# Order and placement of the three partial products of each weight tile in a float32 decoder layer

## The reference

```python
def decoder_layer(x, pos, ret_S0, rwkv_S0, shift0, p):
    x = x + 0.5 * swiglu(rms_norm(x, p['norm_ffn1']), p['ffn1_w_gu'], p['ffn1_w_down'])
    h = rms_norm(x, p['norm_mix'])
    z = h @ p['w_in']
    ...
    ret_S, o_ret = retention_branch(zq, zk, zv, zg, pos, ret_S0)
    rwkv_S, o_rwkv, shift = rwkv7_branch(zs, shift0, rwkv_S0, p)
    merged = (jax.nn.sigmoid(zgr) * (o_ret @ p['w_ret_o'])
              + jax.nn.sigmoid(zgw) * (o_rwkv @ p['w_rwkv_o']))
    x = x + merged @ p['w_out']
    x = x + 0.5 * swiglu(rms_norm(x, p['norm_ffn2']), p['ffn2_w_gu'], p['ffn2_w_down'])
    return x, ret_S, rwkv_S, shift
```

## Time and profile before

| | us |
|---|---|
| Median of 3 runs | 2866.72 |
| Lowest, highest | 2866.03, 2868.74 |
| The profiled execution | 2868.76 |
| Its span, first to last instruction | 2867.0 |

### The profile page before, as it was taken

How to read it: one execution, slowest core, us unless ns; L and a number is a source line. 1 busy time by engine, 2 the same in 40 slices (tenths; PEclk the granted TensorE clock), 3 DMA queues, 4 the chain that set the end, 5 groups by cost and what they waited for, 6 DMA issues and landing times.

```text
span 2867.0 us, 57289 instructions
## 1 busy us (share of the span) xinstructions
PE 2841.1 (99%) x24662; PEld 2768.5 (97%) x24662; DVE 1564.2 (55%) x1679; ACT 1117.0 (39%) x1121; POOL 107.2 (4%) x144
## 2 busy tenths in 40 slices
PE   9999999999999999999999999999999999999998
PEld 8999999999999999898998999999999999999998
DVE  6444444444567576775865555466544444454454
ACT  5333333333344453544534644233433333333333
POOL 0000000000000002011020010000000000000000
PEclk9999999999999999999999999999999999999999
DMA  5444454444456553635436444555444445444454
GB/s 205 167 163 164 162 171 176 161 171 155 164 186 228 190 186 111 249 131 200 162 139 240 176 154 165 187 203 184 164 172 161 166 161 171 175 162 167 155 169 144
DMA packets 85460, 495.80 MB, mean 173 GB/s; under 512 B 10320, under 2 KB 10496, under 8 KB 44096
## 3 DMA queue, kind: packets, MB, share of 16 engines
q1 hardware_dynamic: 71424, 444.14, 44.0%
q0 software_dynamic: 9280, 32.72, 3.1%
q10 hardware_dynamic: 4608, 16.78, 1.5%
HBM read 462.80 MB, written 30.80 MB: 172 GB/s over the span
## 4 chain that ended last, share of the span: by engine, by line
PE 93%; DVE 3%; ACT 2%; DMA 1%; issue 0%; SPq 0%; ACTq 0%; DVEq 0%; POOLq 0%
PE psum L545 29%; PE psum L546 29%; PE psum L547 29%; PE psum L893 1%; PE psum L709 1%; DVE sb_w_lo L1506 1%; DMA sb_raw<-in_w_wo 0%; DMA sb_raw<-in_gu 0%; PE psum L666 0%; ACT sb_w_hi L1094 0%; DVE sb_w_lo L1512 0%; ACT sb_w_hi L1085 0%; PE psum L906 0%; PE psum L903 0%; PE psum L745 0%
## 5 line engine op out<-in xcount | busy, mean ns | idle before, releaser
L547 PE MATMUL psum<-sb_h,sb_w_lo 128*128 128x288 f32 x4384 | 1297.7, 296 | 0.0
L546 PE MATMUL psum<-sb_h,sb_w_hi 128*128 128x288 f32 x4384 | 1293.9, 295 | 0.0
L545 PE MATMUL psum<-sb_h,sb_w_hi 128*128 128x288 f32 x4384 | 1288.5, 294 | 4.2 <-DVE sb_w_lo L1506 1.7
L1512 DVE TENSOR_TENSOR sb_w_lo<-sb_raw,sb_w_hi 128x2048 fp32r<-128x2048 f32 (+1 forms) x348 | 712.4, 2047 | 713.8 <-ACT sb_w_hi L1085 713.2
L1085 ACT ACTIVATE sb_w_hi<-sb_raw 128x2048 fp32r<-128x2048 f32 (+1 forms) x349 | 600.2, 1720 | 1207.6 <-PE psum L547 1177.5
L545 PEld LDWEIGHTS psum<-sb_h,sb_w_hi 128*128 128x128 f32 x4384 | 828.4, 189 | 28.5 <-issue 19.9
L547 PEld LDWEIGHTS psum<-sb_h,sb_w_lo 128*128 128x128 f32 x4384 | 823.9, 188 | 0.0
L546 PEld LDWEIGHTS psum<-sb_h,sb_w_hi 128*128 128x128 f32 x4384 | 821.5, 187 | 1.3 <-issue 1.0
L547 PE MATMUL psum<-sb_g,sb_w_lo 128*128 128x288 f32 x1408 | 416.8, 296 | 0.0
L546 PE MATMUL psum<-sb_g,sb_w_hi 128*128 128x288 f32 x1408 | 415.4, 295 | 0.0
L545 PE MATMUL psum<-sb_g,sb_w_hi 128*128 128x288 f32 x1408 | 407.0, 289 | 0.0
(11 more groups left out here) (380 smaller groups left out, 2389.0 us busy)
## 6 DMA issues: line engine op xcount, KB each, us to landing
sb_raw<-in_gu SPq DMA_DIRECT2D x175, 1024.0 KB, 4.8
sb_raw<-in_down SPq DMA_DIRECT2D x128, 704.0 KB, 4.1
sb_raw<-in_w_mix SPq DMA_DIRECT2D x72, 1024.0 KB, 4.9
sb_raw<-in_w_gates SPq DMA_DIRECT2D x32, 1024.0 KB, 5.4
sb_s_ret<-in_s_ret POOLq DMA_DIRECT2D x32, 512.0 KB, 8.4
out_ret_s<-sb_s_ret ACTq DMA_DIRECT2D x32, 512.0 KB, 5.4
sb_raw<-in_w_ro SPq DMA_DIRECT2D x16, 1024.0 KB, 4.8
sb_raw<-in_w_out SPq DMA_DIRECT2D x16, 1024.0 KB, 4.8
```

Source lines behind the costliest of these rows:

```text
L545: pe.matmul(out, wh, xh, start=start, stop=False)
L546: pe.matmul(out, wh, xl, start=False, stop=False)
L547: return pe.matmul(out, wl, xh, start=False, stop=stop)
L1512: dve.tensor_tensor(w_lo[:, slot, 0:cols], raw[:, slot, 0:cols], w_hi[:, slot, 0:cols].bitcast(F32), ALU.subtract).then_inc(lo_made, 2)
```

## The change

Two things are changed. In `products` the last two matmuls change places: line 546 is now low weights by high inputs, line 547 high weights by low inputs. And the tensors are placed anew: low weights 192 bytes from the high ones modulo 256 instead of 128, high inputs 80 bytes instead of 144, and with them low inputs 208 instead of 16. To use the gaps, `h` now stands before `w_lo`, and `dend` and `gains` have moved. The tensors from `x` and `o_ret` on shift by 32 bytes up, those behind an `align` by 64 bytes down; `or_hi` stands at 160 or 32, `or_lo` at 192 or 64.

```diff
-LINES, APART = 256, 144
+LINES, APART, LOW_APART = 256, 80, 192
...
         w_hi = sb("w_hi", [P, 2, BLK], F32R)
-        eps_c = sb("eps_c", [P, 3])
-        first_root = eps_c[:, 2:3]
-        own = sb("own", [P, SB])
...
-        align(4 * T % LINES)
+        eps_c = sb("eps_c", [P, 3])
+        first_root = eps_c[:, 2:3]
+        own = sb("own", [P, SB])
+        h_hi, h_lo = halves_of("h", KT)
+        dend = sb("dend", [P, 2, 4 + SB])
+        align(LOW_APART)
         w_lo = sb("w_lo", [P, 2, BLK], F32R)
-        h_hi, h_lo = halves_of("h", KT)
+        gains = sb("gains", [P, 4, KT])
         mean_w = sb("mean_w", [P, P])
         head_w = sb("head_w", [P, P], F32R)
         ident = sb("ident", [P, P])
-        gains = sb("gains", [P, 4, KT])
         arena = place[0]
...
-        dend = sb("dend", [P, 2, 4 + SB])
...
                 pe.matmul(out, wh, xh, start=start, stop=False)
-                pe.matmul(out, wh, xl, start=False, stop=False)
-                return pe.matmul(out, wl, xh, start=False, stop=stop)
+                pe.matmul(out, wl, xh, start=False, stop=False)
+                return pe.matmul(out, wh, xl, start=False, stop=stop)
```

## The result

| | before | after |
|---|---|---|
| median, us | 2866.38 (2866.03 to 2868.74, 4 runs) | 2901.43 (2887.57 to 2913.79, 4 runs) |
| profiled execution, us | 2868.76, span 2867.0 | 2887.57, span 2885.8 |
| ratio | | 1.0119, 95% interval 1.009 to 1.0148 |

What follows compares the result with a forecast made beforehand. TensorE was taken to bound the kernel: 6560 tiles by their step, plus some 290 us. One 6.667 ns step less over 5730 tiles, 38 us, from 2866.7 gave 2828 us; whole range 2790 to 2906.

Steps and rivals of the forecast that it cites:

- The bound: Whole kernel: TensorE sets the time, 6560 weight tiles of three products times their step, plus some 290 us untouched.
- the small ones: Matmuls touched by moved small buffers and shifted mixing buffers: left at their cost, some 3 us either way.
- the first rival: Products: inputs' high, high, low cycle and places modulo 64 are kept, so 393.3 ns and 2867 us stay; chance 0.22.
- The reload: Rival, products: losing the repeated load of high weights leaves none short, 400 ns a tile, 2905 us; chance 0.15.
- the looser lost lock: Rival, products: tiles fall to the other layout's 398.4 ns, 29 us slower, 2896 us; chance 0.13.
- The forecast: Products: three different distances make a tile one step shorter, 387 ns, saving 38 us to 2828 us; chance 0.42.
- no longer meet alike: Products: input streams and loads, all 144 bytes apart before, meet at 144, 80 and 208, giving 127 + 127 + 133 ns.
- The argument from distances alone: Products: the step follows from distances modulo 256 between input stream and load; addresses matter by about 5 ns a tile.
- The grid: Products: a pattern repeating every tile moves in steps of 6.667 ns, so only 386.7, 393.3 or 400.0 ns can occur.
- The tiles between small matmuls: Mixing steps: half of 1152 tiles counted as following the pattern, making 5730 tiles in all.
- The loads: Weight loads of 187, 188, 189 ns should change with the product beside them if the streams' meeting is the cause.
- wrong in kind: Test of the whole forecast: it fails if the step varies within the stretch or the difference lies outside the three lines.

Runs made afterwards that it cites:

- the bare streams: Kernels without the layer: TensorE alone runs bursts of three-product tiles at listed addresses; before's placement took 393.3 ns a tile, the changed kernel's 395.5 or 395.6 in the first sweep.
- old/192/80: Changed kernel with the old order of products, keeping low weights at 192 and high inputs at 80; 2890.71 us, ratio 1.0081.
- new/32/16: Changed kernel in its new order, with low weights at 32 and high inputs at 16; 2849.98 us, ratio 0.9934.
- 2 of 20 bursts: Products alone without the layer, changed kernel's order and placement, 20 bursts after varying pauses: 395.5 or 395.6 ns in 15, 406.7 in 3, 386.7 in 2.
- the shift of 16 bytes: Products alone without the layer, before's placement with all four operands moved together by 16 bytes: 396.7 ns a tile in 19 bursts, 396.6 in 1.
- the second trace of the changed kernel: Changed kernel run again unchanged, also called the repeat; 2921.16 us, ratio 1.0151, profiled span 2935.2 us.
- old/48/144: Kernel before, old order and high inputs at 144, with low weights at 48 instead of 128 and small buffers moved; 2860.44 us, ratio 0.9975.
- 448 single bursts: Products alone without the layer, one burst for each of 448 placements in both orders, low inputs 128 bytes on: 148 at 400.0 ns, 106 at 393.3, 88 at 396.7.

## Why the prediction was wrong, step by step

- **The bound held.** The time is 6560 tiles by their step; nothing else moved. 18.5 of the 18.8 us lie in the three lines, and all other matmuls together moved by 0.3 us, within the 3 that I gave the small ones (line 964 gained 0.9 us, line 590 lost 0.7). VectorE and ScalarE did not change.
- **That addresses modulo 256 bytes matter held, and the first rival fell.** Its condition (places modulo 64 and the inputs' cycle are kept, so nothing changes) was met to the letter, and the step moved by 2.3 to 13.4 ns. The sentence of the Trainium skill that I had set beside it (SBUF — State Buffer, section Who interferes with whom: "PE and ACT never wait on anyone") is about one engine holding up another, and the bare streams neither confirm nor refute it, since no other engine works in them. What they refute is what I drew from it, that no placement would change a step: with every other engine idle, TensorE's step for the same three products goes from 386.7 to 406.7 ns by where its operands lie.
- **The reload fell, though the sign and size of its rival came near.** It gave 2905 us, and the looser lost lock 2896; measured was 2901. But its reason (a product is short because of the reload) is refuted from both sides: old/192/80 has the reload and no product at 289, new/32/16 lacks it and is faster than before. A time that fits is no evidence for the reason.
- **The forecast failed at the step that it called its weakest**: that three different distances would put the tile at 386.7. No row stood behind "no longer meet alike". The pattern exists at this placement (127 to 131 ns gaps, 2 of 20 bursts), but two others exist as well, and the kernel's long stretches fell into those every time in two traces: 395.6 ns in one, 406.7 in the other, where the sum had 386.7. The argument from distances alone fails too, by the shift of 16 bytes.
- **The grid was right in its unit and wrong in its period.** I took the pattern to repeat every tile, so that only 386.7, 393.3 and 400.0 could occur. It may repeat over three tiles (178 x 6.667 / 3 = 395.6) or two (390.0), so steps a third or a half of 6.667 ns apart are open, and small losses with them. What I read as "equal durations, hence one stable lock" was a property of before's placement, not of TensorE: before is one of those with a single pattern.
- **The tiles between small matmuls were mis-sized.** I counted half of 1152 as in the pattern. The 1568 tiles of the lora columns, the mixing steps and the gates paid 5.4 ns each, more than twice the 2.3 of the long stretches, and 8.5 of the 18.8 us are theirs. Short stretches at 386.7, 395.6 and 406.7 ns all occur there, so I take it that every interruption starts the choice anew, but no run separates that from what a tile loses while it settles.
- **The loads move, but not with the product beside them.** In the second trace of the changed kernel the loads of lines 545 and 546 take 193 ns, where the first trace has 188. The load of line 545 runs beside the 305 ns of line 547, that of line 546 beside the 295 ns of line 545, that of line 547 beside the 296 ns of line 546. So loads and products change together with the pattern, which fits the meeting of the two streams, but two products of nearly one length have loads of 193 and 187 ns beside them.
- **I would be wrong in kind if the step varied within the stretch**, the prediction said. Within the stretch of 440 to 700 us it did not; it varied between executions instead, which none of its cases held. The range of 2790 to 2906 covers the median, but not the runs of 2911 and 2914, and not 2921 of the repeat.

Two things stay open. What in the chip makes the patterns no run shows; that a common shift of 32 bytes is harmless and one of 16 is not is the only hint. And what a start or a disturbance has to be like to lead into one pattern or another I could not read from the traces.

## What to carry to other kernels

Where weight loads and input streams alternate on TensorE, read the step of an undisturbed stretch and the minimum and maximum of each product: these show at once whether the operands' places cost something, and a bare stream of a few dozen products at the same distances gave the step of the long stretches in all kernels here but one (406.7 of old/48/144). Try a placement in many bursts with different starts and take one that has a single pattern: here a lower step with a second pattern beside it (386.7 and 406.7) was worth less than a steady 390.0. Then check the whole kernel's trace, which can hold patterns that the bursts lack. And before a time of one trace is explained, take a second trace of the same kernel: here it differed by 49 us.

## What the hardware showed beyond that

- A tile of three fp32r products of 288 columns with 128 columns of weights settles at 386.7 to 406.7 ns, by placement and start alone, at full granted clock (1.00 in the stretches that the rows above come from). The Trainium skill (TensorE: Matmul & The Clock Gate, section Back-to-back issue gap) has N / 2.4 + 2.5 ns for an isolated product at full clock; an estimate from that is 122.5 ns here or 367.5 for three. No placement here settled at that; the least was 386.7. For a stream of loads and products the same section gives about 131 ns each at 512 columns; here 512 columns took 700 ns for three, 233 each.
- Most settled totals are multiples of 6.667 ns, 16 columns at 2.4 GHz: 58, 59, 60 and 61 of them for one tile, 117 for two, 178 for three. Of the 448 single bursts 425 fit a multiple over one to four tiles within 0.12 ns a tile.
- Width counts in jumps at a fixed place: 8 more columns (272 to 280) cost 16.7 ns in three products, the next 8 at most 3.3, and 16 more (288 to 304) 27 to 30.
- Halving the columns of the weight load saves some 5 ns in three products (397.4 to 392.0 in the mean of 16 places), so most of what they take above 360 ns does not go with the load's length.
- A pattern can hold for 1054 tiles, the whole of a long stretch, through the waits at every block of weights.
